# Last layer of a two-block network: q and k products and attention of head pairs in one loop

## The reference, cut to what matters

```python
def stick_breaking_block(q_blk, k_ctx, v_ctx, q0):        # per head, d = 64
    z = jnp.einsum('bthd,bshd->bhts', q_blk, k_ctx) * (SB_HEAD_DIM ** -0.5)
    before = jnp.arange(s_len)[None, :] < (q0 + jnp.arange(tq))[:, None]
    log_keep = jnp.where(before, jax.nn.log_sigmoid(-z), 0.0)
    csum = jnp.cumsum(log_keep, axis=-1)
    weights = jnp.where(before, jnp.exp(jax.nn.log_sigmoid(z) + csum[..., -1:] - csum), 0.0)
    return jnp.einsum('bhts,bshd->bthd', weights, v_ctx)

def stick_breaking_layer(h, norm_w, w_in, w_out):         # 16 heads
    u = rmsnorm(h, norm_w)
    q, k, v, g = jnp.split(u @ w_in, 4, axis=-1)
    ...                                                   # o = the blocks above
    o = o * jax.nn.silu(g)
    return h + o @ w_out

# then: rmsnorm(h, final_norm) of the 256 tokens is the output
```

## Time and profile before

| | us |
|---|---|
| time, median of 3 runs (lowest, highest) | 1300.44 (1299.69, 1301.47) |
| the profiled execution: its own time | 1303.09 |
| its span, first to last instruction | 1301.2 |
| TensorE busy | 1127.3 (87%) |
| VectorE busy | 629.3 (48%) |
| ScalarE busy | 453.3 (35%) |

### The profile page before, as it was taken

One profiled execution on the slowest core, in us unless ns is written; L12 is line 12 of the kernel. 1 busy time (PEld: TensorE's weight loads), 2 busy tenths in 40 slices (PEclk: granted clock), 3 DMA queues, 4 the chain that ended last, 5 costly groups with the idle time before them and its releaser, 6 DMA issues.

```text
span 1301.2 us, 19504 instructions
## 1 busy us (share of the span) xinstructions
PE 1127.3 (87%) x8166; PEld 841.6 (65%) x8166; DVE 629.3 (48%) x1168; ACT 453.3 (35%) x835; POOL 78.4 (6%) x118
## 2 busy tenths in 40 slices
PE   5899999999996756799999675669999999999898
PEld 3677758896842312269984231326999779999856
DVE  4655876656520201156753010114885489655584
ACT  3535534322410000044341000002664666533473
POOL 3000224540000000000000000000100000000000
PEclk8999999999997888799999888879999999999999
DMA  9937765119989999995878999999345305454100
GB/s 326 330 129 262 285 230 199 66 43 391 421 353 422 420 421 421 415 325 194 324 305 343 422 419 422 422 417 353 130 150 175 130 1 184 141 194 165 46 2 32
DMA packets 104187, 339.17 MB, mean 261 GB/s; under 512 B 7849, under 2 KB 10774, under 8 KB 81574
## 3 DMA queue, kind: packets, MB, share of 16 engines
q1 hardware_dynamic: 97408, 334.51, 66.3%
q10 hardware_dynamic: 6694, 3.43, 1.0%
HBM read 336.88 MB, written 1.05 MB: 260 GB/s over the span
## 4 chain that ended last, share of the span: by engine, by line
PE 60%; DMA 13%; SPq 11%; DVE 10%; ACT 4%; issue 2%; ACTq 0%; DVEq 0%
PE bank L712 8%; PE bank L714 8%; PE bank L713 8%; SPq L1409 7%; DMA weight_ring<-in_w_up_dram 5%; PE bank L1065 4%; SPq L1420 4%; PE bank L612 3%; DVE arena L2137 3%; DMA arena<-in_w_up_dram 3%; DMA arena<-in_w_gate_dram 3%; PE bank L689 2%; PE bank L570 2%; PE bank L690 2%; DVE weights_low L2137 2%
## 5 line engine op out<-in xcount | busy, mean ns | idle before, releaser
L2137 DVE TENSOR_TENSOR weights_low<-weight_ring,weights_high 128x1024 fp32r<-128x1024 f32 x150 | 183.5, 1225 | 146.5 <-ACT weights_high L1591 146.1
L1591 ACT ACTIVATE weights_high<-weight_ring 128x1024 fp32r<-128x1024 f32 x150 | 158.2, 1056 | 187.9 <-PE bank L714 173.6
L712 PE MATMUL bank<-input_high,weights_high 128*128 128x272 f32 (+1 forms) x672 | 195.3, 291 | 4.7 <-DVE input_low L2137 2.3
L714 PE MATMUL bank<-input_high,weights_low 128*128 128x272 f32 (+1 forms) x672 | 192.0, 286 | 0.0
L713 PE MATMUL bank<-input_low,weights_high 128*128 128x272 f32 (+1 forms) x672 | 191.5, 285 | 0.0
L2137 DVE TENSOR_TENSOR arena<-arena,bank 128x512 f32<-128x512 f32 (+1 forms) x38 | 24.6, 651 | 224.4 <-PE bank L1065 211.0
L712 PEld LDWEIGHTS bank<-input_high,weights_high 128*128 128x128 f32 x672 | 126.7, 189 | 9.1 <-issue 4.9
L714 PEld LDWEIGHTS bank<-input_high,weights_low 128*128 128x128 f32 x672 | 126.9, 189 | 0.0
L713 PEld LDWEIGHTS bank<-input_low,weights_high 128*128 128x128 f32 x672 | 126.7, 189 | 0.1
L712 PE MATMUL bank<-raw_high,weights_high 128*128 128x272 f32 (+1 forms) x320 | 92.5, 289 | 2.0 <-DVE weights_low L2137 2.0
L714 PE MATMUL bank<-raw_high,weights_low 128*128 128x272 f32 (+1 forms) x320 | 91.2, 285 | 0.0
(11 more groups left out here) (467 smaller groups left out, 1969.6 us busy)
## 6 DMA issues: line engine op xcount, KB each, us to landing
weight_ring<-in_ada_w_dram SPq DMA_DIRECT2D x24, 2048.0 KB, 10.2
weight_ring<-in_w_gate_dram SPq DMA_DIRECT2D x16, 2048.0 KB, 24.6
arena<-in_w_down_dram SPq DMA_DIRECT2D x16, 2048.0 KB, 32.7
arena<-in_w_gate_dram SPq DMA_DIRECT2D x12, 2048.0 KB, 21.4
arena<-in_w_up_dram SPq DMA_DIRECT2D x12, 2048.0 KB, 33.0
weight_ring<-in_w_up_dram SPq DMA_DIRECT2D x12, 2048.0 KB, 27.7
weight_ring<-in_even_w_in_dram SPq DMA_DIRECT2D x9, 2048.0 KB, 9.2
expert_slots<-in_w_up_dram SPq DMA_DIRECT2D x8, 2048.0 KB, 32.6
```

The costliest lines, as they stand in the source:

```text
L712: pe.matmul(b[:, 0:width], hi[:, k, :], high[:, k, t0:t0 + width], start=k == 0, stop=False)
L714: mm = pe.matmul(b[:, 0:width], lo[:, k, :], high[:, k, t0:t0 + width], start=False, stop=k == KD - 1)
L1591: act.activation(WHI[:, j % 2], quarter_of(j), ACT.Copy).then_inc(weights_high, 1)
L2137: return dve.tensor_tensor(out_, a, b, op)
```

## The change

The weight chunks of the last layer come in another order: g, g, v, v, q0, k0, q1, k1. Nothing is computed differently and no product is dropped. The eight g quarters go first, then the eight v quarters. Then one loop over the head pairs p: quarter q p, `stick_turn(p-2)`, `stick_scores(p-1)`, quarter k p, `stick_out(p-2)`. The rows of v are turned in the loop's first pass. The output product's first quarters stand between the last pairs' steps, and each pair's output is split by itself (`split_input(OS, T, p, 1)`). WS and TAKE move to where v and the ada partials were, since the raw input must stay in place to the end of the loop. The load of the final norm's row moves behind the loop on ScalarE's queue. The quarter's body becomes a function, `quarter_product`, and that of the output product `final_quarter`.

```diff
-        KEEP, TAKE, WS = at(17024, 3, STICK + 1), at(18276, 3, STICK), at(19524, 4, STICK)
+        KEEP, WS = at(17024, 3, STICK + 1), at(7424, 4, STICK)
+        TAKE = (at(9088, STICK), at(23076, STICK), PART[:, 0:STICK])
...
-        stream += [cols(odd_w_in_2[0], 512 * i) for i in range(8)]
+        stream += [cols(odd_w_in_2[0], 512 * i) for i in (6, 7, 4, 5, 0, 2, 1, 3)]
...
-                product(W_OD + j, 4 * j, T, v_open, v_close, "q", new_input=j == 0, after=last_norm_part(6, L2, SQ3) if j == 0 else None,
+                product(W_OD + j, 4 * j, T, v_open, v_close, "g", new_input=j == 0, after=last_norm_part(6, L2, SQ3) if j == 0 else None,
...
-                product(W_OD + 2 + j, 4 * j, L2, v_open, v_close, "k", high=RAWHI, low=RAWLO)
-                product(W_OD + 4 + j, 4 * j, L2, v_open, v_close, "v", high=RAWHI, low=RAWLO)
-                product(W_OD + 6 + j, 4 * j, T, v_open, v_close, "g", t0=META, high=RAWHI, low=RAWLO)
+                product(W_OD + 2 + j, 4 * j, L2, v_open, v_close, "v", high=RAWHI, low=RAWLO)
+
+            def value_rows(pieces):
+
+                pe.wait_ge(vector_drained, mark[("v", KD - 1)])
+                for i, kh in pieces:
+                    t0, r = SRC[i]
...
+                pe.wait_ge(vector_drained, mark[("k", p)])
...
-            stick_scores(0)
-            stick_scores(1)
+            value_pieces = [(i, kh) for i in range(len(SRC)) for kh in range(2)]
             for p in range(pairs):
-                stick_turn(p)
-                if p + 2 < pairs:
-                    stick_scores(p + 2)
-                stick_out(p)
-            def residual_rows(half, tt, b):
-
+                cn = W_OD + 4 + 2 * (p // 4)
+                quarter_product(cn, p % 4, p, T, v_open, v_close, "q", t0=META, high=RAWHI, low=RAWLO)
+                if p == 0:
+                    value_rows(value_pieces[0:3])
+                if p >= 2:
+                    stick_turn(p - 2)
+                if p >= 1:
+                    stick_scores(p - 1)
+                quarter_product(cn + 1, p % 4, p, L2, v_open, v_close, "k", high=RAWHI, low=RAWLO)
+                if p == 0:
+                    value_rows(value_pieces[3:6])
+                if p >= 2:
+                    stick_out(p - 2)
+
+            residual_rows(0, 0)
+            stick_scores(pairs - 1)
+            residual_rows(0, 1)
+            final_quarter(0, 0)
+            stick_turn(pairs - 2)
+            final_quarter(0, 1)
+            stick_out(pairs - 2)
+            stick_turn(pairs - 1)
+            final_quarter(0, 2)
+            residual_rows(1, 0)
+            stick_out(pairs - 1)
+            residual_rows(1, 1)
+            final_quarter(0, 3)
+            for m in range(4):
+                final_quarter(1, m)
...
-            for _ in range(3 * KD - 2):
-                high()
             for m in range(KD):
                 high()
                 act.wait_ge(vector_drained, mark[("g", m)])
                 act.activation(SGT[:, m, :], SGT[:, m, :], ACT.Silu).then_inc(stick_gates, 1)
-            act.dma_start(FNORM, final_norm_2.rearrange("(o n) -> o n", o=1).broadcast_to([P, D])).then_inc(final_norm_in, 16)
+            for _ in range(KD - 2):
+                high()
...
+            pairs = SB_H // 2
+            for p in range(pairs):
+                high()
+                if p >= 2:
+                    stick_turned()
+                if p >= 1:
+                    stick_sigmoids(2 * p - 2)
+                high()
+                if p >= 1:
+                    stick_sigmoids(2 * p - 1)
+            act.dma_start(FNORM, final_norm_2.rearrange("(o n) -> o n", o=1).broadcast_to([P, D])).then_inc(final_norm_in, 16)
+            stick_sigmoids(2 * pairs - 2)
+            stick_sigmoids(2 * pairs - 1)
+            high()
+            stick_turned()
+            high()
+            stick_turned()
...
+                drained(tt(OS[:, p, :], b[:, 0:T], SGT[:, p, :], MUL), True)
+                split_input(OS, T, p, 1)
...
+            pairs = SB_H // 2
+            value_pieces = [(i, kh) for i in range(len(SRC)) for kh in range(2)]
+            for p in range(pairs):
+                b = take()
+                drained(stt(QS[:, p, :], b[:, 0:T], 64 ** -0.5, NR6[:, META:L2], MUL, MUL))
+                if p == 0:
+                    value_rows(value_pieces[0:3])
+                split()
+                b = take()
+                drained(tt(KS2[:, p, ::-1], b[:, 0:L2], NR6, MUL))
+                if p == 0:
+                    value_rows(value_pieces[3:6])
+                if p >= 1:
+                    stick_weights(2 * p - 2)
+                split()
+                if p >= 2:
+                    stick_o(p - 2)
+                if p >= 1:
+                    stick_weights(2 * p - 1)
+            stick_weights(2 * pairs - 2)
+            stick_weights(2 * pairs - 1)
+            split()
+            stick_o(pairs - 2)
+            split()
+            stick_o(pairs - 1)
+            for _ in range(4):
                 split()
```

More of the change, by code:

```diff
@@ L696, in first_product, with quarter_product @@
                 released[cn] = (weights_split, len(quarters)) if i else (scalar_filled, done)
+            def quarter_product(cn, m, tile, width, opener, closer, names, ready=None, t0=0, high=XHI, low=XLO):
+                j = len(quarters)
+                pe.wait_ge(weights_split, j + 1)
+                b = opener()
+                hi, lo = WHI[:, j % 2], WLO[:, j % 2]
+                for k in range(KD):
+                    if ready is not None:
+                        pe.wait_ge(*ready(k))
+                    pe.matmul(b[:, 0:width], hi[:, k, :], high[:, k, t0:t0 + width], start=k == 0, stop=False)
+                    pe.matmul(b[:, 0:width], hi[:, k, :], low[:, k, t0:t0 + width], start=False, stop=False)
+                    mm = pe.matmul(b[:, 0:width], lo[:, k, :], high[:, k, t0:t0 + width], start=False, stop=k == KD - 1)
+                done = closer(mm, (names, tile))
+                quarters.append((cn, m, scalar_filled if closer is s_close else vector_filled, done))
+                if m == 3:
+                    released[cn] = (weights_split, len(quarters))
@@ L707, in product @@
[L707 to L714, removed]
@@ L715, in product @@
[L715 to L716 removed]
+                    quarter_product(cn, m, mt + m, width, opener, closer, names, ready if m == 0 else None, t0, high, low)
                     if after is not None:
                         after(mt + m)
[L719 removed]
             warm(4)
@@ L1344, in residual_rows @@
                               start=k == 0, stop=False)
[L1346 to L1374, removed]
@@ new lines, in final_quarter @@
+            def final_quarter(half, m):
+                cn, j = W_OD + 8 + half, len(quarters)
+                pe.wait_ge(weights_split, j + 1)
+                hi, lo = (w[:, j % 2].rearrange("p (k a) n -> p k (a n)", k=2) for w in (WHI, WLO))
+                for tt in range(TT):
+                    b, t = rows[half, tt], slice(tt * P, tt * P + P)
+                    for i in range(2):
+                        k = 2 * m + i
+                        if half == 0 and tt == 0:
+                            pe.wait_ge(input_split, KD * (n["inputs"] - 1) + k + 1)
+                        pe.matmul(b[:, :], XHI[:, k, t], hi[:, i, :], start=False, stop=False)
+                        pe.matmul(b[:, :], XHI[:, k, t], lo[:, i, :], start=False, stop=False)
+                        mm = pe.matmul(b[:, :], XLO[:, k, t], hi[:, i, :], start=False, stop=m == 3 and i == 1)
+                    if m == 3:
+                        v_close(mm, ("final", half, tt))
+                if m < 3:
+                    mm.then_inc(weights_used, 1)
+                    n["used"] += 1
+                quarters.append((cn, m) + ((weights_used, n["used"]) if m < 3 else (vector_filled, n["v"])))
+                if m == 3:
+                    released[cn] = (weights_split, len(quarters))
@@ L2793, in _ @@
                 b = take()
-                drained(stt(QS[:, m, :], b[:, 0:T], 64 ** -0.5, NR6[:, META:L2], MUL, MUL))
-                split()
-            for m in range(KD):
-                b = take()
-                drained(tt(KS2[:, m, ::-1], b[:, 0:L2], NR6, MUL))
+                drained(tt(SGT[:, m, :], b[:, 0:T], NR6[:, META:L2], MUL))
                 split()
```

53 lines of the change are left out of this document (18 added, 35 removed).

## The result

The changed kernel takes 1303.66 us (median of 20 runs, 1302.05 to 1306.27), the one before, beside it, 1302.21 (20 runs, 1299.69 to 1303.34). The ratio is 1.0016 with a 95% interval of [1.001, 1.0022]: 1.3 to 2.9 us slower, 2.1 in the middle (the two medians alone differ by 1.45). The prediction had +1.6. Its 1302.1 was counted from 1300.44, the median of three runs; beside the changed kernel the one before took 1302.21, so only the differences can be compared. They can be told from no change, which the prediction had doubted for a difference of this size.

What follows compares the result with a forecast made beforehand. TensorE bounds the last layer, but a chain through VectorE and TensorE would bind the new loop: 11.83 us of new waits less 10.19 removed gives +1.6, from 1300.44 to 1302.1 us, range 1291.0 to 1309.0.

Steps and rivals of the forecast that it cites:

- The bill of before: Last layer of the kernel before: TensorE's waits and slow-clock time sum to 10.19 us, all the change can win there.
- 0.66 + 2.09: Kernel before: 0.66 us extra in v's second twelve transposes, 2.09 at the first two scores, the latter put to the clock.
- The chain: Loop: five VectorE steps take 5.98 us from k p's end to stick_turn, against 4.22 of TensorE work; 1.76 wait, 11.45 period.
- last weights: VectorE's last step before stick_turn, weights of head 2p-1: scan and wait 1.05 us, product 0.59.
- The second wait: Scores in the loop wait for ScalarE's copy of the first turned bank; hidden, otherwise about 0.35 us a pass.
- The tail: Behind k7: waits of 0.16 us at the second residual bank and 0.67 at the last; the old 1.63 idle goes.
- The 0.16 at the second bank: Tail: the second bank of residual rows waits 0.16 us for the drain of pair 5, 3.72 against 3.56.
- The clock: TensorE in the loop: forecast assumed 2.4 GHz holds; a fall behind the turns' waits was named as what could spoil it.
- rival B: Slower: clock falls behind the turns' waits, 1307 us at three of six, 1316 at all with longer stretches; chance 0.25.
- The threshold: TensorE's clock falls from waits of about 1.9 us, as after 1.92 and 1.90 but not 1.84.
- The rule on transposes: Turns in the loop: transposes not counting as array work, every wait would bring the low clock, about 1312 us.
- rival C: Faster: VectorE's work is hidden, the loop runs at TensorE's 9.69 us a pass, 1291.1 to 1293 us; chance 0.14.

Runs made afterwards that it cites:

- The version without waits in the loop: Changed kernel, with both heads' weights made before the k quarter and ScalarE copying turned weights ahead of the next q quarter's high part; 1291.78 us, ratio 0.9929.
- g first alone: Kernel before with only the quarter order changed to g, v, q, k; attention and output product stay behind the products; ratio 0.9993.
- first head early: Changed kernel, but VectorE makes the weights of head 2p-2 before it takes the k quarter; 1297.52 us, ratio 0.9966.
- output behind: Changed kernel, but VectorE handles the output of pair p-2 behind the weights of head 2p-1 instead of ahead; ratio 0.9985.
- first pass only: Changed kernel, but VectorE makes the weights of head 0 ahead of the k quarter in pass 1 alone; ratio 1.0005.
- the two with more sums: Changed kernel with two unused VectorE sums per pass, either behind k's drain and split (ratio 1.0133) or behind the split after q's drain (1.002).
- more on the chain: Changed kernel with two unused VectorE sums per pass between the split behind k's drain and the output of pair p-2; 1318.88 us, ratio 1.0133.

## Why the prediction was right

*The bill of before* (10.19 us). The version without waits in the loop gains 9.2 in time and 8.45 in the layer, with a tail that still waits for 1.27; that makes 10.5 or 9.7, and the sum stands. The share put to the clock does not. "g first alone" has the second twelve transposes and the wait behind them in 3.57 us at the full clock, against 3.58 before, and the first scores to the first turn in 5.04 against 5.94. So of 0.66 + 2.09 the clock cost 0.90, and the rest is time in which TensorE would have waited for VectorE anyway. The fused loop removes both kinds, so the forecast did not depend on the split.

*The chain.* Each step as it was priced, against the rows of the pass above: notice and drain 0.53, measured 0.46 (1203.05 to 1203.51); weights 1.56, measured 1.56; split 1.15, measured 1.13; output 1.04, measured 1.13 (the one-tile cast takes 0.29, not 0.20); last weights 1.64, measured 1.64; 0.06. Sum 5.98, measured 5.98: small errors cancelled. The pass of 11.45 was exact. Taking 1.13 or 0.8 out of this chain shortens the pass by as much (1.11 and 0.8), putting 0.84 in lengthens the wait by as much, and the same work in VectorE's idle time costs 0.07. That is shown, by five kernels (first head early, output behind, first pass only, and the two with more sums).

*The second wait* behind it, at the scores, was foreseen as hidden and came out as soon as the first was gone, at 0.52 to 0.58 instead of 0.35.

*The tail.* 0.67 for the last drain: 0.60 from start to start (0.53 in the bracket). The 0.16 at the second bank did not show.

*The clock* is the part that the forecast did not have. It held the clock at 2.4 GHz; in the profiled execution it fell once, at the first wait, and cost 1.56. That is one of rival B's six falls, near its price (1.7). 1.64 + 1.56 = 3.2 is the 3.18 of the layer: there the forecast chain is right and the forecast sum is half of what was measured. That the time shows 2.1, nearer to the forecast, is not to the prediction's credit. Why it does is open. The fall may come in some executions only: one execution of the changed kernel was profiled, and other waits of this size bring it in some profiles and not in others (last section). But the difference in time lies 0.6 to 1.6 us below that in the layer in eight of the ten experiments too, with falls and without (first head early: -4.4 against -3.39), so that the one profiled execution of the kernel before may as well have had a short layer.

*The threshold* of about 1.9 us that rival B gave does not hold as a threshold. In the changed kernel's own profile the wait of 1.92 was not followed by a fall, and a wait of 2.12 was at one place and not at another.

*The weight stream*, the moved buffers and the final norm's row were priced at nothing, and no wait on a load shows in the loop.

*The rule on transposes* (the Trainium skill, TensorE: Matmul & The Clock Gate, Part 4: PE-mode transpose), from which the prediction drew that every wait ahead of a turn would bring the low clock, and 1312 us: five of six such waits brought none, all of 1.50. The measurement decides against it in this strength. It does not show that transposes count in full; with 0.84 more of waiting all six brought it.

What the prediction lacked is the next step. It named VectorE's written order as the only thing between its forecast and rival C, and that order was free to change: the weights of head 2p-2, and with ScalarE's sigmoids those of 2p-1, needed nothing from the k quarter.

## What to carry to other kernels

When two phases are interleaved, add up the chain through the engines from one phase's last product back to its next use, in written order, and compare it with the work that stands between: a loop in which every engine is idle for a part of each pass is bound by such a chain. Then look in it for work that waits only because it stands behind a wait, and put that ahead; here three moves of a few lines turned +2.1 us into -9.2. A wait that goes uncovers the next one, so the gain of each is to be counted to there. And a price put to the clock is to be taken from the same stretch at the full clock: a wait that would have been there anyway hides part of it.

## What the runs showed of the hardware

In this loop the 1.2 GHz level came behind the longer waits of TensorE and behind no shorter one. Idle times in the bracket of 0.37 to 1.57: no fall in over thirty; 1.94 (twice), 2.01, and six of 2.33 to 2.78: a fall each time. A fall mostly lasted 3.4 us, twice 6.8 (before at 1230, and the last one with more on the chain), and cost 1.45 to 1.67 a pass. So the price of a wait has a step in it: 0.84 us more of waiting cost 2.4 us a pass.

Between the two it is not settled by the length of the wait. Three waits of the layers ahead stand in all twelve profiles with the same matmuls around them, and only the executions differ. The one of 1.84 was never followed by a fall; the one of 1.92 was in 5 of 12; and one of 2.12, which comes twice in each profile, was in 8 of 24. Here it is in the kernel before (first two rows) and in the changed one, near 354 us, where their work is the same:

```profile
354.84 0.39 PE L1000 MATMUL bank<-ident,small 128*16 128x128 f32 x2 [2.12 <-DVE small L2137]
354.00:356.00 2.00, 1.16 (x7) 0.98 (x8) 1.25 (x6) 2.00 (x5) 0.00 (x0) 1.00 0.99 414
```

```profile
354.38 0.59 PE L1007 MATMUL bank<-ident,small 128*16 128x128 f32 x2 [2.12 <-DVE small L2179]
354.00:356.00 2.00, 1.62 (x5) 1.31 (x6) 1.21 (x6) 2.00 (x4) 0.00 (x0) 0.59 1.00 418
```

So a wait of 1.9 to 2.1 us was followed by a fall in some executions and not in others, whatever the kernel, and one profile does not tell which.
